# The ten opening weight panels get raw buffers of their own, four loads in flight, and new lists for ACT and DVE

## The reference

```python
def first_block(x, mem, ...):
    mem_n = rms_norm(mem, norm_mem)              # 256 x 1024
    h = rms_norm(x, norm_mix[l])                 # 512 x 1024
    proj = h @ w_in[l]
    ...
    x = x + memory_cross_attention(rms_norm(x, norm_cross[l]), mem_n, ...)

def memory_cross_attention(h, mem_n, wq, wkv, q_g, k_g, wo):
    kv = mem_n @ wkv                             # needs mem alone, not x
    ...
```

## Time and profile before

| | us |
|---|---|
| median of 3 runs | 1653.4 |
| runs | 1652.73, 1653.4, 1659.86 |
| the profiled execution | 1660.93 |
| its span in the profile | 1658.9 |
| PE busy | 1614.4 (97%) |
| DVE busy | 940.9 (57%) |
| ACT busy | 664.1 (40%) |
| POOL busy | 201.9 (12%) |

### The profile page before, as it was taken

The page is one execution under the profiler, slowest core; times in us unless marked ns, Lnnn a source line. Parts: engine busy times, 40 slices in busy tenths (PEclk is TensorE's granted clock), DMA queues, the critical chain, the costliest instruction groups (busy, mean ns, idle before and its releaser), DMA issues.

```text
span 1658.9 us, 21628 instructions
## 1 busy us (share of the span) xinstructions
PE 1614.4 (97%) x7524; PEld 1324.8 (80%) x7524; DVE 940.9 (57%) x1319; ACT 664.1 (40%) x974; POOL 201.9 (12%) x119
## 2 busy tenths in 40 slices
PE   6999999989999999999999999999999999999997
PEld 5888789768778888888878888888888888888886
DVE  4569969765474422543367766666546544444333
ACT  5513346353654322432245444554224443443221
POOL 2767658300000000000000000000000000000000
PEclk9999979999999999999999999999999999999998
DMA  7421100113122222222223333322222222222332
GB/s 274 163 76 68 54 1 1 64 39 114 39 74 91 102 88 101 89 102 90 93 82 92 99 99 101 92 92 99 102 101 89 102 89 101 89 100 82 99 97 76
DMA packets 45665, 149.50 MB, mean 90 GB/s; under 512 B 4784, under 2 KB 5936, under 8 KB 45616
## 3 DMA queue, kind: packets, MB, share of 16 engines
q1 hardware_dynamic: 42240, 139.90, 25.3%
q10 hardware_dynamic: 3376, 8.95, 1.4%
HBM read 146.47 MB, written 2.10 MB: 90 GB/s over the span
## 4 chain that ended last, share of the span: by engine, by line
PE 87%; DVE 8%; ACT 2%; issue 1%; DMA 1%; SPq 0%; DVEq 0%; ACTq 0%
PE acc L625 79%; DVE c_acc L2062 1%; DMA raw<-panels_a 1%; PE acc L871 1%; DVE d_score_a L2157 1%; PE acc L911 1%; DVE qkv L1989 1%; DVE tok L2200 1%; DVE w_lo L1930 0%; PE acc L940 0%; PE acc L700 0%; PE acc L965 0%; DVE d_score_a L2203 0%; ACT w_hi L1363 0%; DVE qkv L2119 0%
## 5 line engine op out<-in xcount | busy, mean ns | idle before, releaser
L625 PE MATMUL acc<-h_hi,w_hi 128*128 128x512 f32 x1248 | 496.7, 398 | 4.8 <-DVE w_lo L1938 2.3
L625 PE MATMUL acc<-h_hi,w_lo 128*128 128x512 f32 x1248 | 493.6, 395 | 0.0
L625 PE MATMUL acc<-h_lo,w_hi 128*128 128x512 f32 x1248 | 490.3, 393 | 0.0
L1938 DVE TENSOR_TENSOR w_lo<-raw,w_hi 128x1024 fp32r<-128x1024 f32 (+2 forms) x241 | 281.6, 1171 | 80.1 <-ACT w_hi L1370 59.5
L1370 ACT ACTIVATE w_hi<-raw 128x1024 fp32r<-128x1024 f32 (+2 forms) x241 | 242.2, 1008 | 174.7 <-PE acc L625 94.5
L625 PEld LDWEIGHTS acc<-h_hi,w_hi 128*128 128x128 f32 x1248 | 236.3, 189 | 59.3 <-issue 4.2
L625 PEld LDWEIGHTS acc<-h_lo,w_hi 128*128 128x128 f32 x1248 | 236.4, 189 | 53.5 <-issue 1.2
L625 PEld LDWEIGHTS acc<-h_hi,w_lo 128*128 128x128 f32 x1248 | 236.2, 189 | 50.6
L625 PE MATMUL acc<-u_hi,w_lo 128*128 128x512 f32 x256 | 100.9, 394 | 0.0
L2341 DVE TENSOR_TENSOR x<-x,acc 128x512 f32 x32 | 22.0, 688 | 138.6 <-PE acc L625 138.2
L625 PE MATMUL acc<-u_lo,w_hi 128*128 128x512 f32 x256 | 100.4, 392 | 0.0
(11 more groups left out here) (392 smaller groups left out, 2395.3 us busy)
## 6 DMA issues: line engine op xcount, KB each, us to landing
raw<-panels_a SPq DMA_DIRECT2D x112, 512.0 KB, 3.2
raw<-panels_b SPq DMA_DIRECT2D x68, 512.0 KB, 3.2
raw<-mix SPq DMA_DIRECT2D x48, 448.0 KB, 3.2
raw<-mix SPq DMA_DIRECT2D x16, 512.0 KB, 3.5
raw<-down SPq DMA_DIRECT2D x16, 384.0 KB, 3.0
raw<-down SPq DMA_DIRECT2D x16, 320.0 KB, 2.8
x<-xT ACTq DMA_DIRECT2D x4, 1024.0 KB, 9.7
x_rows<-xN ACTq DMA_DIRECT2D x2, 1024.0 KB, 10.4
```

The source lines that it names most:

```text
L625: mm = e.matmul(out, w[:, w_at:w_at + wn], a, start=first and n == 0, stop=last and n == 2)
L1938: TTn(lo, raw, k.w_hi[:, ahead.slot(w)].bitcast(F32), ALU.subtract).then_inc(k.s_split_done, 1)
```

## The change

The ten lead panels are loaded to a buffer of their own, `raw_lead`, ten panels long, so no load of them waits for a split. SP issues the first four at once and each further one when the load four before it has landed (`FLIGHT = 4`, four semaphores). Behind them it issues panels 10 and 11 to the two buffers of `raw` with no wait. The streaming loop starts at panel 12. On ACT and DVE the lists of the opening are written anew: panel 2 is rounded between the squares of the first and of the second half of `x_rows`, panels 3, 4 and 5 before the first `normalised`, and the panels 6 to 9 lie between the normalised tiles; on DVE the remainders of panels 0 to 2 stand before the reciprocal, of 3 to 5 before the wait for `x`, and of 6 to 9 behind xn0, xn2, xn4 and xn6. The starting credit of `s_split_done` is given by DVE instead of POOL. The semaphores of the two feed-forward parts are shared (`s_hid_*`), with the counts of the second continuing those of the first. The diff, without the renamed semaphores:

```diff
+FLIGHT = 4
+    k.raw_lead, _ = sb("raw_lead", LEAD * PANEL, at=r0 + 32 * 1024)
+    k.lead_landed = [sem(f"lead_landed{n}") for n in range(FLIGHT)]
@@ sync_program
-    pan = Panels()
-    first = True
+    for n in range(LEAD):
+        if n >= FLIGHT:
+            e.wait_ge(k.lead_landed[n % FLIGHT], 16 * (n // FLIGHT))
+        e.dma_start(til(k.raw_lead, n, w=PANEL), d.panels_a[n]).then_inc(k.lead_landed[n % FLIGHT], 16)
+    pan = Panels(LEAD)
+    for j in range(RAW):
+        e.sem_inc(k.landed[j], 16 * (LEAD // RAW))
+    for _ in range(RAW):
+        e.dma_start(k.raw[:, pan.unsplit()], d.panels_a[pan.at()]).then_inc(k.landed[pan.n % RAW], 16)
+        pan.step()
@@ scalar_program
     def round_lead():
-        e.wait_ge(k.landed[lead.n % RAW], lead.landed())
+        e.wait_ge(k.lead_landed[lead.at() % FLIGHT], 16 * (lead.at() // FLIGHT) + 16)
         e.wait_ge(k.s_panel_used, lead.at(1))
-        A(k.w_hi[:, lead.slot()], k.raw[:, lead.unsplit()], ACT.Copy).then_inc(k.s_weights_hi, 1)
+        A(k.w_hi[:, lead.slot()], til(k.raw_lead, lead.at(), w=PANEL), ACT.Copy).then_inc(k.s_weights_hi, 1)
...
     x_squares(0)
     x_squares(1)
+    round_lead()
+    keys(0)
     e.wait_ge(k.s_ld_x_rows[1], 16)
     x_squares(2)
     x_squares(3).then_inc(k.s_x_sums, 1)
...
     round_lead()
-    keys(0)
+    keys(1)
     round_lead()
-    keys(1)
-    normalised(0)
     keys(2)
     round_lead()
+    keys(3)
+    normalised(0)
+    round_lead()
     normalised(1)
+    normalised(2)
     round_lead()
-    keys(3)
-    normalised(2)
     normalised(3)
+    normalised(4)
+    load_mem_rows()
     round_lead()
-    normalised(4)
     normalised(5)
+    normalised(6)
     round_lead()
-    normalised(6)
     normalised(7)
-    round_lead()
-    round_lead()
@@ vector_program
     rest_lead()
     rest_lead()
+    rest_lead()
     invert(1, tok(TOK_RX, TT), TT)
+    rest_lead()
     rest_lead()
     rest_lead()
     e.wait_ge(k.s_pe_once, PE_ONCE["x_row"])
...
-        if m in (0, 2, 4, 6, 7):
+        if m in (0, 2, 4, 6):
             rest_lead()
-    rest_lead()
```

## The result

The changed kernel is slower, by about 1% in the first comparison and by half of that in two later ones. In the first comparison its median was 1672.11 us (four runs, 1668.14 to 1679.61) against 1653.18 for the kernel before (four runs, 1652.73 to 1659.86): ratio 1.0108, 95% interval 1.0072 to 1.0144. Forecast was 1659.4 within 1649 to 1665: the sign was right, but 1672.11 lies above the range. Of the difference between the kernels the forecast had too little, against the first comparison by two thirds, against the later ones by a third.

What follows compares the result with a forecast made beforehand. PE was taken to bound the kernel, busy 97% of the span, with the end of `rest` as yardstick. x landing at 35.0 plus 20.5 ends `rest` at 55.5 against 49.49: 1653.4 + 6.0 = 1659.4 us, range 1649 to 1665.

Steps and rivals of the forecast that it cites:

- the sign: Whole kernel: the forecast was slower, by 6.0 us over the median of the kernel before.
- the round: Opening, after x lands: one xn pair, second h_hi, w_hi and w_lo repeat every 4.4 us, against 3.8 before.
- the drips of `rest`: PE does `rest` piecemeal, its last three tiles over 5 us; the forecast sum counted no clock loss there.
- the base and spread: Whole kernel: the forecast counted from the median 1653.4 us of three runs, which spanned 7.1 us.
- The queue and x: Opening loads: queues share packets equally, so x lands behind twelve panels at 35.0 instead of 24.6, bounds 32.5 to 36.5.
- Rival 1: Opening loads: x lands as before, near 24.6, so `rest` ends 4.4 us earlier, 1649.0 us; chance 0.15.
- Rival 3: Opening loads: x is late by half as much, landing at 29, `rest` ends at 49.5, 1653.4 us; chance 0.13.
- the lists give back 4.3 us: Opening: with the new lists `rest` ends 20.5 us behind x's landing, where before it ended 24.8 behind xn0.
- Rival 2: PE's clock falls after its new gaps; one fall in `rest`'s drips costs 1.7 us, two 3.4: 1661 to 1663; chance 0.22.
- The parts that cost nothing: Memory rows and squares on ACT, POOL's panel 10 before `k1`, shared semaphores: price nought, bounds -0.3 to +0.3 us.

Runs made afterwards that it cites:

- eight: Changed kernel with SP waiting for both halves of x before panel 8, new ACT and DVE lists, earlier broadcast row: 1649.73 us, ratio 0.9964 to the kernel before; repeated 0.9960.
- six panels ahead: Changed kernel, but SP waits for both halves of x before it issues panel 6: 1664.99 us against 1658.2 for the kernel before, ratio 1.0041.
- the second profile of the changed kernel: Changed kernel run again without edit beside the kernel before: 1664.71 us against 1654.68, ratio 1.0058.
- the buffers alone: Changed kernel with ACT's and DVE's lists of before, own buffers and early loads kept: 1667.69 us against 1658.2 for the kernel before, ratio 1.0047.
- the lists alone: Kernel before, each load still waiting for a split, with the new ACT and DVE lists: 1659.68 us against 1658.2, ratio 1.0015.
- rounds ahead: Changed kernel with each ACT round_lead of panels 6 to 9 one normalised group earlier: 1654.50 us against 1654.68 for the kernel before, ratio 1.0001.

## Why the prediction was wrong, and where it was right

The mechanism was right, x behind twelve panels. Three sizes were wrong: the round (4.4 us for 5.0), a fall of the clock in the drips of `rest` that the sum had at nothing (1.6), and the base and spread taken from three runs, which put the result out of the range.

**The queue and x: right.** x was to land at 35.0 and landed at 34.3; the row was to begin at 24 and began at 22.75, after a wait of 3.0 us for 3; xn0 was to start at 34 to 36 and started at 34.35. Equal packets in both queues held with twelve, eight and six panels ahead of x (over 10 to 20, in q1 and q10: 576 and 566 in the second profile of the changed kernel, 567 and 570, 561 and 579), and x landed at 34.3, 30.0 and 26.9. Rivals 1 and 3, x as before or at 29, are out. So is the gain that rival 1 drew from the Trainium skill ("DMA: Bandwidth & Descriptors", Anatomy of one DMA): the page fits its fixed 2 us to loads issued by GpSimd, these are issued by SP and ACT, and with more of them in flight the buffers alone lose 10.1 us at the mark.

**The round: the term that was mis-sized in the opening.** I took 4.4 us and it was 5.0, three times: xn pairs start at 38.20, 43.21 and 48.22, xn7 at 53.25. The pair (1.39) and DVE's wait for w_hi (1.65 for 0.5 + 1.1) were sized rightly. w_lo was not: it took 2.04 instead of 1.48. The reason is POOL, by when its h_lo began. The w_lo of 1.48 began 0.4 before a running h_lo ended, and took 0.25 more than the 1.23 of one alone. In the new rounds ACT delivers two h_hi in a row, POOL runs from 39.68 to 42.21, and the w_lo that begins at 41.24 has 0.97 of it ahead: it took 0.81 more. The same 2.04 to 2.08 come in every run with the new rounds, x late or early, and 1.46 to 1.48 in the buffers alone, with the old lists and x late. So a duration beside another engine's work was carried to a place where that work lies differently. Three rounds of 0.6 more and the 0.2 by which I rounded the sum down (20.5 for 20.7), less 0.7 for an x that landed earlier than 35.0, made `rest` end at 56.05 + 0.7 = 56.8 instead of 55.5. The lists' loss wasn't in my rivals either: "the lists give back 4.3 us" took the distance of xn0 to the end of `rest` as a gain, though the same lists put panel 5 ahead of xn0, which the run of the lists alone shows as 7.5 us of x lying ready. Rival 1's 1649.0 rests on the same error: with x as early as before, the new lists are later than the old, not earlier.

**The clock: a term that the sum had at nothing.** Rival 2 named the drips of `rest` as the place, at 1.7 us, and the forecast left it out. In the profile of after the granted clock falls three times in the opening: between 22 and 28 and between 43 and 48, both ahead of something that PE then waits for, and in the first matmuls behind the last h_lo, where it costs:

```profile
50.00:56.00 6.00, 3.46 (x16) 2.49 (x14) 2.73 (x2) 3.21 (x6) 3.52 (x4) 1.00 0.00 1
56.00:62.00 6.00, 5.95 (x19) 4.75 (x20) 2.48 (x6) 2.46 (x5) 5.92 (x3) 0.72 0.69 224
```

The 27 matmuls behind the last h_lo took 8.06 us there and 6.47 in the second profile of the changed kernel, 1.6 more:

```profile
56.64 6.47 PE acc L633 x27
```

7.3 (56.8 against 49.49) and 1.6 make the 9.0 of the mark, but for 0.1. The fall came in two of three profiles of the changed kernel (8.07 in the third), and in that of six panels ahead. PE's gap ahead of it doesn't settle it: the wait for the last h_lo was 2.6 us in the second profile too, where no fall followed.

**The median: the step that put the result out of the range.** I counted from the median of three runs, 1653.4, and took their spread of 7 for that of the kernel. 31 and 29 and 23 further runs gave 1658.2, 1654.68 and 1655.29, with single runs from 1647 to 1672. The 18.9 us between the first medians are made of 9.0 at the mark, 2.4 behind it (the profiled executions differ by 11.4), and 7.5 by which the profiled execution of before, 1660.93, lay further above its median than that of after, 1672.35, above its own. The last two I put down to where the clock falls in single runs; two repetitions gave 10.0 and 8.5 us in place of 18.9. Against the later medians the first four runs of after lay 7.4 and 8.3 us high (with mean clocks of 0.976 to 0.987), those of before 1.5 to 5.0 low. So the forecast's own error is 3 us, in the opening (1.3 in the end of `rest`, 1.6 in the clock), and the range was too narrow because the spread of single runs is over three times what I put in. The chance of "slower", 0.27, was too low because I expected 6.0 where 8.3 was the bound and 9 to 10 was true. What decides in a single run where the clock falls between 120 and 370 stays open.

**The parts that cost nothing** did so: POOL began panel 10 at 55.95 and was done at 60.3, `k1` wanted it at 64.55; no wait there is in the chain.

## What to carry to other kernels

When the DMA engines are full, an earlier load is taken from another one: count the bytes that stand ahead of the transfer the chain waits for, in packets if two queues share the engines, and hold back by its landing what isn't needed sooner. In a hand-written order that goes back and forth between two engines, let each produce one group ahead of where the other consumes it; that single move was worth 7 us at the mark here. And before a range is set for a small change, ask how far the kernel's own runs spread: three runs showed 7 us of it, nearly a hundred showed 24.

## What the hardware showed that was not expected

Two queues that both hold work get equal numbers of packets whatever their size, so the queue with 4 KB packets gets twice the bytes of the one with 2 KB (67 and 67 packets, 0.27 and 0.14 MB, in the stretch 22 to 23 of the kernel after). A load that comes to an empty queue while the other has a backlog can be slow to begin: in the kernel before, panel 2 was issued at 12.95 and q1 moved nothing over 13 to 16.5 (28 packets over 16 to 17), while q10 had the engines. DVE and POOL hold each other up when both subtract, and the one that begins while the other is at work pays. A w_lo of 128 x 1024 on DVE takes 1.22 to 1.23 us alone or when it begins first, and 1.48, 1.53, 2.04 and 2.27 with 0.40, 0.44, 0.97 and 1.18 us of a POOL subtraction still to run. POOL's h_lo takes 1.27 alone, and 1.80 with 0.65 of a w_lo still to run, as in the kernel before:

```profile
31.78 1.80 POOL L540 TENSOR_TENSOR h_lo<-x,h_hi 128x512 fp32r<-128x512 f32 x1 [0.43 <-ACT h_hi L1403]
```

The h_lo ahead of the w_lo of 2.27 (40.08, rounds ahead):

```profile
39.98 1.28 POOL L548 TENSOR_TENSOR h_lo<-x,h_hi 128x512 fp32r<-128x512 f32 x1
```

In all five the time added is what the other had left, less 0.12 to 0.16 us, so these two subtractions hardly overlap at all. The rounds of 3.50 us with the rounds ahead are about that: a w_lo and two h_lo, 1.23 + 2 x 1.27 = 3.77, less two such overlaps.
